# Pool mixer computed transposed with shifted sums, and attention's value product for two heads at once

## The reference, cut to what matters

```python
def pool_mixer(u, pool_w, pool_scale):          # windows 2, 4, 8, 16, one for each group
    c = jnp.cumsum(jnp.pad(uf, ((0, 0), (1, 0), (0, 0), (0, 0))), axis=1)
    for g, w in enumerate(POOL_WINDOWS):
        lo = jnp.maximum(t + 1 - w, 0)
        cnt = jnp.minimum(t + 1, w).astype(jnp.float32)
        means.append((c[:, 1:, g] - c[:, lo, g]) / cnt[None, :, None])
    y = (jnp.stack(means, axis=2) - uf).astype(u.dtype)
    y = jnp.einsum('btgc,gcd->btgd', y, pool_w).reshape(B, T, D_POOL)
    return y * pool_scale
...
        p = jax.nn.softmax(logits, axis=-1).astype(vs.dtype)
        return jnp.einsum('bhqk,bqkhd->bqhd', p, vs)
...
        h = h + jnp.concatenate([a, p], axis=-1) @ w_out[l]
```

## Time and profile before

| | us |
|---|---|
| median of 3 runs | 1080.71 |
| the profiled execution | 1081.22 |
| its span | 1079.4 |
| PE matmul busy | 1018.6 (94%) |
| PE in the value product | 20.06 |
| DVE / ACT / POOL busy | 706.8 / 463.2 / 215.5 |

### The profile page before, as it was taken

One profiled execution on the slowest core, in us unless ns is written; L12 is line 12 of the kernel. 1 busy time (PEld: TensorE's weight loads), 2 busy tenths in 40 slices (PEclk: granted clock), 3 DMA queues, 4 the chain that ended last, 5 costly groups with the idle time before them and its releaser, 6 DMA issues.

```text
span 1079.4 us, 18647 instructions
## 1 busy us (share of the span) xinstructions
PE 1018.6 (94%) x6499; PEld 913.0 (85%) x6499; DVE 706.8 (65%) x1248; ACT 463.2 (43%) x749; POOL 215.5 (20%) x203
## 2 busy tenths in 40 slices
PE   5989898999689979999999999999999999999997
PEld 4878768888578767899999999999999999999996
DVE  5596414888899968655666556665566655566554
ACT  5543514221277764444444444444444444444442
POOL 2385101477589940000000000000000000000000
PEclk9989869999889999999999999999999999999999
DMA  6533112642402237655555555555554555555553
GB/s 206 173 123 117 40 39 79 195 131 71 122 25 51 74 98 231 200 192 194 191 175 182 190 194 192 175 181 190 194 191 175 184 189 194 192 178 178 191 194 136
DMA packets 68186, 168.07 MB, mean 156 GB/s; under 512 B 6549, under 2 KB 34217, under 8 KB 68153
## 3 DMA queue, kind: packets, MB, share of 16 engines
q1 hardware_dynamic: 67824, 167.56, 46.2%
q10 hardware_dynamic: 328, 0.08, 0.0%
HBM read 163.42 MB, written 4.19 MB: 155 GB/s over the span
## 4 chain that ended last, share of the span: by engine, by line
PE 69%; DVE 2%; issue 1%; ACT 1%; POOL 0%; DVEq 0%; POOLq 0%
PE psum L1430 32%; PE psum L1159 30%; PE psum L1399 5%; PE psum L1350 2%; DVE rr L950 0%; DVE big L898 0%; POOL raw L1128 0%; ACT raw L574 0%; DVE rr L995 0%; DVE big L1020 0%; DVE rr L903 0%; ACT L535 0%; PE psum L1387 0%; ACT rr L606 0%; ACT rr L612 0%
## 5 line engine op out<-in xcount | busy, mean ns | idle before, releaser
L1430 PE MATMUL psum<-rr 128*128 128x512 f32 x1536 | 370.5, 391 | 1.9 <-DVE rr L980 0.9
L1159 PEld LDWEIGHTS psum<-ht,rr 128*128 128x128 f32 x2784 | 348.8, 192 | 8.7
L1159 PE MATMUL psum<-ht,rr 128*128 128x256 f32 x2784 | 352.1, 283 | 0.0
L1430 PEld LDWEIGHTS psum<-rr 128*128 128x128 f32 x1536 | 281.0, 188 | 57.0 <-issue 2.1
L965 DVE TENSOR_TENSOR rr<-raw,rr 128x1024 fp32r<-128x1024 f32 x115 | 141.0, 1226 | 235.6 <-ACT rr L606 235.6
L606 ACT ACTIVATE rr<-raw 128x1024 fp32r<-128x1024 f32 x115 | 121.9, 1060 | 328.0 <-PE psum L1430 324.1
L903 DVE TENSOR_TENSOR rr<-raw,rr 128x1024 fp32r<-128x1024 f32 x112 | 136.5, 1219 | 2.0 <-ACT rr L529 2.0
L529 ACT ACTIVATE rr<-raw 128x1024 fp32r<-128x1024 f32 x112 | 118.8, 1061 | 38.3 <-DMA raw<-in_peer_u_dram 38.2
L950 DVE TENSOR_TENSOR rr<-cst,picks 128x2048 fp32r<-128x2048 f32 x32 | 92.3, 2896 | 4.4 <-ACT picks L570 2.1
L1159 PE MATMUL psum<-rr,ht 128*128 128x256 f32 x672 | 86.5, 292 | 8.5 <-POOL rr L1034 4.2
L1128 POOL TENSOR_TENSOR raw<-rr,picks 128x512 f32<-128x512 f32 x32 | 90.9, 2873 | 18.1 <-DVE rr L950 18.1
(11 more groups left out here) (157 smaller groups left out, 723.9 us busy)
## 6 DMA issues: line engine op xcount, KB each, us to landing
raw<-in_peer_u_dram SPq DMA_DIRECT2D x128, 512.0 KB, 4.0
raw<-in_peer_v_dram SPq DMA_DIRECT2D x128, 512.0 KB, 3.6
big<-in_w_in_dram SPq DMA_DIRECT2D x10, 1024.0 KB, 7.5
big<-in_peer_wq_dram SPq DMA_DIRECT2D x8, 1024.0 KB, 5.6
big<-in_w_out_dram SPq DMA_DIRECT2D x4, 1024.0 KB, 5.1
up_kept<-gel SPq DMA_DIRECT2D x16, 128.0 KB, 3.8
gel<-up_kept SPq DMA_DIRECT2D x16, 128.0 KB, 3.6
big<-in_x_dram SPq DMA_DIRECT2D x2, 512.0 KB, 4.0
```

The lines of the kernel that those rows point to most:

```text
L1159: i = pe.matmul(dst, lhs(a, k), rhs(b, k), start=(n == 0), stop=(n == 3 * DK - 1))
L1430: i = pe.matmul(psum[:, 4 + 2 * t + n, :], g_sp[:, s, x, t * P:(t + 1) * P], v_sp[s][:, y, n * 512:(n + 1) * 512], start=(first and m == 0 ...
```

## The change: what it does, and the diff

The pool chunks 9 and 10 are projected the other way round (`project_pool`): 128 weight columns are stationary, and all 272 tokens move, which needs the tokens in one array `h_all` (meta tokens first). The result has channels on the partitions and tokens along the row. Sums over 2, 4, 8 and 16 tokens are six shifted additions on POOL; four operations on DVE scale and subtract, and the band matmuls, their constants and the DMA for them go. The low part of chunk 7 moves on POOL ahead of the second query tile.

The value product takes two heads at once: 128 stationary columns (the values of both heads) and 256 moving columns (both heads' probabilities), 20 matmuls. Of each result two of four blocks are used (`cat_part`), and high and low parts are written by two operations each. The meta chunk is now multiplied with all 128 rows, so that the rest of `zv` and of `pt` is zeroed on POOL. DVE takes over three of five copies of transposed probabilities, and the stage is ordered anew.

```diff
+        h_all = sb("h_all", [P, 2, DK, T], F32R)
+        hm, ht = h_all[:, :, :, 0:META], h_all[:, :, :, META:T]
...
+        def cat_part(t, j):
+            return psum[j * HD:(j + 1) * HD, 4 + 2 * t:6 + 2 * t, :].rearrange("p b (a j q) -> p (b a) j q", a=2, j=2)[:, :, j, :]
...
             sp.wait_ge(d_rel, 2)
-            sp.dma_start(band, const[:, K_BAND:N_CONST].rearrange("p (a g t) -> p a g t", a=3, g=4)).then_inc(ld_band, 16)
...
+            def keep_pool(c):
+                for n in range(2):
+                    act.wait_ge(z_done, z_after(c) - 1 + n)
+                    act.activation(zp[:, 2 * (c - 9) + n, :], psum[:, 3 * (c % 2) + n, 0:T], ACT.Copy).then_inc(z_ev, 1)
...
             split_w(N_IN)
+            keep_pool(N_IN - 1)
             for t in range(2):
                 act.wait_ge(d_max, t + 1)
...
+            keep_cat(0)
+            act.wait_ge(p_tpad, 2)
+            for n, (c, b, r) in enumerate(((2, 0, META), (3, 2, P))):
+                act.wait_ge(pe_pt, n + 3)
                 act.activation(pt[0:r, c].rearrange("p (b h) q -> p b (h q)", b=2), psum[0:r, b:b + 2, :],
                                ACT.Copy).then_inc(pt_ev, 1)
...
+            probs(0)
+            dve.wait_ge(p_sum, 2)
+            for g, total in enumerate((sum_a[:, 0], sum_b[:, 0], sum_a[:, 2], sum_b[:, 2])):
+                dve.scalar_tensor_tensor(yt[:, g, :], total[:, META:T], 1.0 / WINDOWS[g], zp[:, g, META:T], ALU.mult, ALU.subtract)\
+                   .then_inc(d_y, 1)
+            dve.wait_ge(p_tpad, 2)
+            keep_probs(1, 0, 0, META)
+            keep_probs(2, 1, 2, P)
+            probs(1)
+            dve.wait_ge(pe_y, 1)
             dve.tensor_tensor(p32, psum[:, 6:8, :].rearrange("p b (g t) -> p (b g) t", t=SEQ),
                               gains[:, 16:20].unsqueeze(2).to_broadcast([P, 4, SEQ]), ALU.mult).then_inc(d_p32, 1)
+            cat_low(0)
+            keep_probs(5, 4, 0, P)
...
+            def shifted_add(dst, src, n, done):
+                pool.tensor_tensor(dst[..., 2 * n - 1:T], src[..., 2 * n - 1:T], src[..., n - 1:T - n], ALU.add).then_inc(done, 1)
...
+            def project_pool(s):
+                for n in range(2):
+                    product(psum[:, 3 * s + n, 0:T], lambda a, k: w_sp[:, s, a, k, n * P:(n + 1) * P],
+                            lambda b, k: h_all[:, b, k, :], z_done)
...
-                for h in range(NH):
-                    lo = HD * (h % 2)
-                    for n, (c, vt, r) in enumerate(chunks):
-                        i = pe.matmul(psum[lo:lo + HD, CAT_BANK[t], (h // 2) * P:(h // 2 + 1) * P], zv[0:r, vt, h * HD:(h + 1) * HD],
-                                      pt[0:r, c, h, :], start=(n == 0), stop=(n == len(chunks) - 1))
+            def attend(t, chunks):
+                for a in range(PAIRS):
+                    for n, (c, vt) in enumerate(chunks):
+                        i = pe.matmul(psum[:, 4 + 2 * t + a // 2, (a % 2) * SEQ:(a % 2 + 1) * SEQ], zv[:, vt, a * P:(a + 1) * P],
+                                      pt[:, c, 2 * a:2 * a + 2, :].rearrange("p h q -> p (h q)"), start=(n == 0), stop=(n == len(chunks) - 1))
                 i.then_inc(pe_cat, 1)
```

More of the change, by code:

```diff
@@ L58 @@
 OUT0, WQ0 = N_IN, N_IN + N_OUT
[L60 to L61 removed]
+K_ID, K_IOTA, K_COS, K_SIN = 0, 128, 256, 448
+N_CONST = 640
 def by_vector(c):
@@ L236, in layer @@
         d_xs = sem("d_xs")
+        p_zpad, p_tpad, p_sum, d_y, d_pt = (sem(n) for n in ("p_zpad", "p_tpad", "p_sum", "d_y", "d_pt"))
         e_up, e_gel, a_late = sem("e_up"), sem("e_gel"), sem("a_late")
@@ L452, in _ @@
                                    psum[:, b0:b1, KOFF[t]:KOFF[t] + KEYS[t]], ACT.Relu).then_inc(a_rel, 1)
-            for c in range(5, N_IN - 1):
+            for c in range(5, N_IN - 2):
+                if c == 7:
+                    act.wait_ge(p_zpad, 1)
                 keep_z(c)
-                if c < N_IN - 2:
-                    split_w(c + 2)
+                split_w(c + 2)
                 if c == 6:
@@ L801, in _, with probs @@
                 dve.tensor_reduce(stat[:, 128 + 8 * t:136 + 8 * t], lg, AX.X, ALU.max, negate=True).then_inc(d_max, 1)
-            for t in range(2):
+            def probs(t):
                 k = KEYS[t]
@@ L816, in _ @@
             split_lo(12)
-            for t in range(2):
-                dve.wait_ge(cat_hi, t + 1)
-                dve.tensor_tensor(ht[:, 1, 0:4, t * P:(t + 1) * P], psum[:, CAT_BANK[t], :].rearrange("p (a q) -> p a q", a=PAIRS),
-                                  f(ht[:, 0, 0:4, t * P:(t + 1) * P]), ALU.subtract).then_inc(cat_lo, 1)
+            cat_low(1)
             for c in range(OUT0, WQ0):
@@ L1039, in _ @@
             split_lo(1)
+            pool.memset(zv[:, 2, :], 0.0).then_inc(p_zpad, 1)
             split_lo(5)
@@ L1068, in _ @@
                 pool.wait_ge(p_qk, t + 1)
-            split_lo(7)
+                if t == 0:
+                    split_lo(7)
+            pool.wait_ge(d_rel, 2)
+            for c in (0, 2):
+                pool.memset(pt[:, c], 0.0).then_inc(p_tpad, 1)
             pool.wait_ge(a_kst, 3 * NH)
@@ L1291, in _ @@
                 i.then_inc(pe_pt, 1)
-            for t in range(2):
-                chunks = ((0, 2, META), (1, 0, P)) if t == 0 else ((2, 2, META), (3, 0, P), (4, 1, P))
-                pe.wait_ge(pt_ev, 2 if t == 0 else 5)
-                for h in range(NH):
-                    lo = HD * (h % 2)
-                    for n, (c, vt, r) in enumerate(chunks):
-                        i = pe.matmul(psum[lo:lo + HD, CAT_BANK[t], (h // 2) * P:(h // 2 + 1) * P], zv[0:r, vt, h * HD:(h + 1) * HD],
-                                      pt[0:r, c, h, :], start=(n == 0), stop=(n == len(chunks) - 1))
-                i.then_inc(pe_cat, 1)
+            def attend(t, chunks):
[3 more added lines that the diff above has]
+                                      pt[:, c, 2 * a:2 * a + 2, :].rearrange("p h q -> p (h q)"), start=(n == 0), stop=(n == len(chunks) - 1))
+                i.then_inc(pe_cat, 1)
+            pe.wait_ge(d_log, 4)
+            pe.wait_ge(z_ev, z_after(N_IN - 1))
+            pe.wait_ge(d_prob, 1)
+            turn_probs(0, META, 0, 0)
+            turn_probs(0, P, META, 2)
+            pe.wait_ge(ld_band, 16)
+            pe.wait_ge(d_y, 4)
+            for g in range(4):
+                i = pe.matmul(psum[:, 6 + g // 2, (g % 2) * SEQ:(g % 2 + 1) * SEQ], poolw[:, g, :], yt[:, g, :], start=True, stop=True)
+            i.then_inc(pe_y, 1)
+            pe.wait_ge(d_pt, 2)
+            attend(0, ((0, 2), (1, 0)))
+            pe.wait_ge(d_prob, 2)
+            turn_probs(1, META, 0, 0)
+            turn_probs(1, P, META, 2)
+            pe.wait_ge(pt_ev, 1)
+            turn_probs(1, P, META + P, 0)
+            pe.wait_ge(d_p32, 1)
+            pe.wait_ge(pt_ev, 2)
+            pe.wait_ge(d_pt, 3)
+            attend(1, ((2, 2), (3, 0), (4, 1)))
             pe.wait_ge(pc_lo, 1)
@@ L1476, in constants @@
             c[0:r, at + n * HD + HD // 2:at + (n + 1) * HD] = b[first:first + r]
-    band = np.zeros((P, 3, 4, P), np.float32)
-    for g, w in enumerate((2, 4, 8, 16)):
-        for t in range(P):
-            for s in range(t - w + 1, t + 1):
-                if s >= 0:
-                    band[s, 0, g, t] += 1.0 / w
-                else:
-                    band[P + s, 1, g, t] += 1.0 / w
-                    band[META + s, 2, g, t] += 1.0 / w
-            band[t, 0, g, t] -= 1.0
-    c[:, K_BAND:] = band.reshape(P, -1)
     return c
```

91 lines of the change are left out of this document (40 added, 51 removed).

## The result

The changed kernel takes 1061.47 us (median of 4 runs, 1061.19 to 1063.7) against 1081.14 us of the kernel before on the same chip (4 runs, 1080.68 to 1082.5): a ratio of 0.982, with a 95% interval from 0.980 to 0.984, or 19.7 us less. The profiled execution took 1061.5 us, with a span of 1059.7 us and a mean granted clock of 0.983.

What follows compares the result with a forecast made beforehand. PE, with matmuls in flight for 94% of the span, was taken as the bound; what counts is how much earlier `w_out` ends. 1081.22 - 11.6 - 2.1 = 1067.5, median 0.5 lower: 1067 us, range 1058 to 1076.

Steps and rivals of the forecast that it cites:

- rival A: `y` operations win over POOL's low part (-4.6), clock survives chunk 8's stall (-2.1): 1060 us; chance 0.27.
- Low part of chunk 7: Chunk 7 runs 69.6 to 78.4 without idle; DVE's low part of chunk 8 slips about 0.7 us.
- What is late next: Chunk 8 waits for DVE's low part: PE idle 3.5 us, 2.1 for low clock; of 4.2 us only 0.3 left.
- 2.5 to 4.5 named as a sign: Sign of being right: PE idles 2.5 to 4.5 us before chunk 8, released by DVE line 662.
- Pool chunks: Chunks 9 and 10, transposed: 6.2 us instead of 8.75, gain 2.5 each; chunk 10 starts at 107.1.
- The chain over `y`: Bands' 7.3 us go, but sums, POOL's low part and copies delay the last product to 138.6: gain -3.1.
- The product of tile 1: Last value product: 24 records of 256 columns at 0.22, 5.2 us, ends 143.8 against 155.44; gain 11.6.
- `w_out`: Clock up after a dense product: 23.2 us against 25.3, gain 2.1; not gained if the clock is low at its start.
- At nothing: ... the re-laid tokens: Band DMA, third memset, re-laid tokens and meta copies were priced at nothing.
- B: PE's short bursts stay at 1.2 GHz: tile 0 2.5 more, tile 1 5.4 more, `w_out` loses 2.1: 1077; chance 0.20.
- C: Slower: as B, with the low clock going on through `w_out`, 39.7 instead of 23.2: 1091 us; chance 0.04.
- D: No difference: a transfer or wait behind `w_out` takes the gain back, 1081 us; chance 0.04.

Runs made afterwards that it cites:

- `undo_lo7`: Changed kernel with POOL's low part of chunk 7 back behind both query tiles: 1062.53 us, ratio 0.983 to the kernel before.
- `no_mixer`: Kernel before plus padded meta rows, 272-column token rows starting at column 16, and chunk 7's low part moved; bands stay: 1059.6 us, ratio 0.9775.
- `attn_only`: Kernel before with the value product for two heads at once and split copies, meta chunk still 16 rows: 1079.37 us, 0.9956, in two groups.
- `per_head`: Changed kernel with one matmul for each head in the value product again, meta chunk still 128 rows: 1057.45 us, ratio 0.9782 to the kernel before.
- `pad_only`: Kernel before with values and probabilities of the meta rows zero-padded to 128 rows, one matmul per head: 1066.13 us, ratio 0.9852.
- `per_head16`: Changed kernel with one matmul per head and 16 rows again for the meta chunk: 1071.81 us, ratio 0.99 to the kernel before.
- `lay_both`: Kernel before with only the token array changed: rows of 272 instead of 256 columns, tokens starting at column 16: 1074.66 us, ratio 0.9933.

## Why the prediction came out as it did

The range held the time. The number is nearer to rival A's 1060 than to the forecast's 1067, but neither of A's conditions came true: the waits and the clock in the edited stage were those of the forecast. Of the 5.5 us between forecast and result only about 1.3 lie in that stage.

1. **Low part of chunk 7: right.** Chunk 7 starts without idle. DVE's additions beside POOL's second query tile took 10.55 us for seven instead of 8.83, so DVE's low part of chunk 8 slipped by 1.7 us, not 0.7.
2. **What is late next: right.** PE was idle 4.59 us before chunk 8 (3.5 forecast, and just outside the 2.5 to 4.5 named as a sign), released by line 662; the clock fell (0.57 in the window from 82 to 86 us), and chunk 9 started at 92.27 (92.6). 0.3 us was forecast for the part; chunk 9 started 0.6 us earlier than before, and `undo_lo7` gives 0.2 to 1.2.
3. **Pool chunks: right.** 6.22 and 6.32 us for 6.2; chunk 10 from 106.88 (107.1).
4. **The chain over `y`: right, its links about 1 us early.** Sums ended near 119.0 (119.9), POOL's low part held a DVE operation for 4.74 us, `y` was done at 124.8 (126.2), `pool_w` ran at the lower clock for 3.75 us (3.2), tile 0's product from 128.50 for 4.29 (129.4 for 4.5), the last product from 137.63 (138.6). That the waits eat most of what the bands and the shorter chunks give is what `no_mixer` shows (1.6 us left from chunk 9 to `w_out`). The price of the low part was set at 4.6, and its move brought 4.3.
5. **The product of tile 1: right in its time, wrong in its reason.** 5.42 us for 5.2. But the step gave the gain to the shape ("24 records of 256 columns"), and read in the earlier trace rows that 80 records at 0.25 us are slow for 128 columns. The row says `16*64`, one of two forms that it holds: 32 of the 80 records are of 16 rows, among 48 of 128 rows. `attn_only`, `per_head`, `pad_only` and `per_head16` show that the zeros beside the meta rows are the gain, and that two heads at once cost 2.3 us more in the last product, 2.6 us by the end of `w_out` (3.5 counted from chunk 9), and by the ratios some 4 us in all. The time came out right by luck: the rate of 0.22 us was read from records that all had 128 rows, and the new product's have them too, only because the change pads the meta chunk with zeros, to which the step gave no part in the gain. Nearly half of what padding gives in the product is clock, which the step did not separate. The Trainium skill has both halves of this and I weighed neither: the drain named above, and (same page, "Theoretical Speedup") that weights of at most 64 columns can run up to twice as fast as two tiles. 0.064 us for 64 columns of weights against 0.226 for 128 agree with it: the ratio is 3.5, where twice the moving columns and that rule give at most 2 x 2.
6. **`w_out`: right.** 23.24 us for 23.2.
7. **"At nothing: ... the re-laid tokens": wrong, and the main miss.** The term measured 5.8 us in the trace of the changed kernel, and 0.67% (7.3 us, interval 5.2 to 9.2) alone in `lay_both`. The mistake was to count a layout as bookkeeping because it adds no instruction, though 24 matmuls in each block of an idle-free loop read that operand. "The expert stages behind it are not edited" was true of their lines and not of their data.

The sum: `w_out` ended 15.0 us earlier, where 13.7 were forecast (11.6 + 2.1). The stages up to 387 us gave back 1.1 net (a transpose group at the full clock gained, a stretch at the lower clock in the gate stage lost), and the expert blocks added 5.8, which makes 19.7.

Of the rivals, A failed at both its conditions. B was right that the bursts run at the lower clock up to 130 us, which the forecast had in its prices, and wrong that it would go on: at 132 us the granted clock is 1.00. C and D did not occur.

## What to carry to other kernels

When a change alters several things in one matmul (shape, rows, layout), take each away alone before naming what helped: here the named part, two heads at once, cost 2.5 to 4 us, the other named part, the new mixer, brought 1.6 in its stage, and a by-product, the zero rows, brought 15. A count of records and a mean per record hide a mix of forms; split the row by form before calling a shape slow. And where a loop is bound by PE with no idle time, a change in how its operands lie in memory is a change of the loop: 2% of one group of 24 matmuls was a third of the whole gain. And two traces of the same code parted by 1 us early on, with the clock; compare a stage from its own start before giving a difference of that size to an edit.

## What was unexpected of the hardware

- Matmuls with 16 rows of weights between ones with 128 rows, all 64 columns wide, cost 0.157 us a record at 2.4 GHz (one in three with 16 rows) and 0.31 at 1.2 GHz (every second one); on 128 rows, 0.062 to 0.064 at 2.4 GHz. The extra stands at the changes, in both directions.
- Records with 64 columns of weights and 128 rows ran in two interleaved series, each with 0.109 us from one to the next (`pad_only`, `per_head`).
- The same 24 matmuls took 3.04 us with the moving operand in rows of 256 words from column 0, 3.01 with rows of 272, 2.99 with an offset of 16 words, and 2.98 with both.
- Two POOL memsets of 128 x 1024 took 0.96 us each (2 us for both were taken), and DVE's search operations beside them (0.29, 0.42 and 0.64 us) kept their lengths.
